# Two transformer-like blocks in one kernel: layer edges rearranged (broadcast wait, late tiles, first units in two parts)

## The reference

```python
def second_block(x, pre_norm_w, post_norm_w, even_w_in, even_w_out, odd_w_in, ...):
    for layer in range(DEPTH):
        h = rms_norm(x, pre_norm_w[layer])
        if layer % 2 == 0:
            y = even_mixer(h, even_w_in[e], even_w_out[e])
        else:
            y = odd_mixer(h, odd_w_in[o], odd_w_out[o], ...)
        x = x + rms_norm(y, post_norm_w[layer]).astype(x.dtype)
    return x
```

## Time and profile before

| | |
|---|---|
| median of 3 runs | 2850.13 us (2848.59 to 2850.41) |
| profiled execution, its own time | 2852.63 us |
| its span | 2850.8 us |
| TensorE matmul busy | 2599.5 us, 91%, 16315 instructions |
| VectorE busy | 1450.0 us, 51% |
| ScalarE busy | 1227.6 us, 43% |
| GpSimd busy | 229.9 us, 8% |
| mean granted TensorE clock | 0.961 |

### The profile page before, as it was taken

The page is one execution under the profiler, slowest core; times in us unless marked ns, Lnnn a source line. Parts: engine busy times, 40 slices in busy tenths (PEclk is TensorE's granted clock), DMA queues, the critical chain, the costliest instruction groups (busy, mean ns, idle before and its releaser), DMA issues. The chain is left out here.

```text
span 2850.8 us, 42051 instructions
## 1 busy us (share of the span) xinstructions
PE 2599.5 (91%) x16315; PEld 2107.5 (74%) x16315; DVE 1450.0 (51%) x2412; ACT 1227.6 (43%) x2306; POOL 229.9 (8%) x300
## 2 busy tenths in 40 slices
PE   5999999999999999988889899999998989997677
PEld 4778987777777989877768688785335877887666
DVE  5122266666656414577766424413776655247642
ACT  6112344454544311366653522213666647225642
POOL 1000020010020000001100000000000100007500
PEclk8999999999999999999999999999999999996779
DMA  7430000000122010100003220101001211010012
GB/s 259 167 128 23 32 18 1 1 1 1 60 82 104 31 45 31 60 2 2 1 7 113 74 89 1 60 30 45 1 1 52 105 41 45 30 64 26 1 46 80
DMA packets 71125, 139.55 MB, mean 49 GB/s; under 512 B 2729, under 2 KB 37954, under 8 KB 70802
## 3 DMA queue, kind: packets, MB, share of 16 engines
q1 hardware_dynamic: 53856, 75.89, 7.8%
q0 software_dynamic: 16832, 60.90, 5.8%
q10 hardware_dynamic: 242, 0.07, 0.0%
HBM read 120.08 MB, written 16.78 MB: 48 GB/s over the span
## 5 line engine op out<-in xcount | busy, mean ns | idle before, releaser
L163 ACT ACTIVATE WORK<-PS 128x512 f32<-128x512 f32 (+5 forms) x307 | 151.6, 494 | 634.4 <-PE PS L794 396.0
L794 PE MATMUL PS<-HT_R,W_R 128*128 128x512 f32 (+1 forms) x864 | 328.5, 380 | 0.0
L792 PE MATMUL PS<-WORK_R,W_R 128*128 128x512 f32 (+1 forms) x640 | 245.1, 383 | 28.0 <-issue 17.9
L793 PE MATMUL PS<-WORK_R,W_R 128*128 128x512 f32 (+1 forms) x704 | 266.5, 379 | 0.0
L163 DVE TENSOR_REDUCE SM<-PS 128x1 f32<-128x1280 f32 (+3 forms) x180 | 199.1, 1106 | 94.8 <-PE PS L1087 49.4
L909 PE MATMUL PS<-WORK_R,HT_R 128*128 128x512 f32 x544 | 217.1, 399 | 21.1 <-DVE W_R L163 20.1
L794 PE MATMUL PS<-W_R,WORK_R 128*128 128x256 f32 (+3 forms) x704 | 215.2, 306 | 0.0
L911 PE MATMUL PS<-W_R,HT_R 128*128 128x512 f32 x544 | 214.1, 394 | 0.0
L910 PE MATMUL PS<-WORK_R,MIXT_R 128*128 128x512 f32 x544 | 213.9, 393 | 0.0
L793 PE MATMUL PS<-W_R,HT_R 128*128 128x256 f32 (+2 forms) x688 | 206.2, 300 | 0.0
L163 ACT ACTIVATE HT<-PS 128x512 f32<-128x512 f32 (+7 forms) x211 | 123.7, 586 | 186.4 <-PE PS L840 111.9
(11 more groups left out here) (291 smaller groups left out, 5682.8 us busy)
## 6 DMA issues: line engine op xcount, KB each, us to landing
MIXT<-in_w_mod POOLq DMA_DIRECT2D x8, 2048.0 KB, 8.4
x_scratch<-WORK POOLq DMA_DIRECT2D x24, 512.0 KB, 2.9
WORK<-x_scratch POOLq DMA_DIRECT2D x24, 512.0 KB, 3.5
W<-in_odd_w_in SPq DMA_DIRECT2D x12, 1024.0 KB, 5.2
W<-in_o_w_in SPq DMA_DIRECT2D x10, 1024.0 KB, 5.1
W<-in_even_w_in SPq DMA_DIRECT2D x5, 2048.0 KB, 8.9
W<-in_w_mod SPq DMA_DIRECT2D x4, 2048.0 KB, 21.2
WORK<-in_x POOLq DMA_DIRECT2D x16, 512.0 KB, 8.1
```

What stands on the lines that cost most here:

```text
L163: self.last = Signalled(self, issue(*args, **kwargs))
L792: mm(out, a[0], b_[0], start=k == 0, stop=False)
L793: mm(out, a[1], b_[0], start=False, stop=False)
L794: return mm(out, a[0], b_[1], start=False, stop=k == KT - 1)
```

## The change

Three edits, all in the three `boundary` functions and the first units behind them.

- DVE's wait for `bcast_in` moves from the head of `boundary` to the first tile, behind its wait for x.
- At edge 2, in the last tile's turn, tile five's high and low part and tile six's eviction move between the steps of the last tile; the high parts of tiles six and seven stay ahead of `first` on ACT. At edge 3 on ACT, `first` (the eviction of an l_x unit) moves behind all late tiles.
- The two units over tiles five to eight run as `split_two`: both banks open, first the 256 columns of tiles five and six for both, then those of tiles seven and eight. Part 0 waits for tile six's low part, part 1 for tile eight's. At edge 3 the first two units over tiles one to four are taken one ahead of the last tile's transposes and one behind.

```diff
+            def split_two(b, keys, name, fs, g, bys):
+                c0, _ = TGL[g]
+                banks = [open_unit(pe, key, by) for key, by in zip(keys, bys)]
+                for part in range(2):
+                    c = c0 + 256 * part
+                    h_split(b, c // P + 1)
+                    for f, bank in zip(fs, banks):
+                        for k in range(KT):
+                            slab_split(name, k)
+                            w = slice(f * P, (f + 1) * P)
+                            o = second_high[b] + 512 * k + 256 * part
+                            last = three_passes(bank[:, 256 * part:256 * part + 256], (high_of(name)[:, k, w], low_of(name)[:, k, w]),
+                                                (WORK_R[:, o:o + 256], HTR[:, k, c:c + 256]), k)
+                        if part:
+                            finish_unit(last)
...
                     x_transposes(b, tiles[-2])
                     first()
                     x_transposes(b, tiles[-1])
+                    if then:
+                        then()
...
             def r_gate_units(n, g):
                 name = ("r_gate", "s_gate")[n // 2]
+                if n == 0 and g:
+                    split_two(2, [(name, r, TGL[g][0]) for r in range(2)], f"{name}0", (0, 1), g, ("act", "act"))
+                    return
...
             def l_x_units(half_n, g):
+                if half_n == 0 and g:
+                    split_two(3, [("l_x", r, TGL[g][0]) for r in range(2)], "l_x0", (0, 1), g, ("dve", "act"))
+                    return
...
-            boundary(3, "r_out", lambda: l_x_units(0, 0))
+            def l_x_first(r):
+                split_t(3, ("l_x", r, TGL[0][0]), "l_x0", r, 0, "act" if r else "dve")
+
+            boundary(3, "r_out", lambda: l_x_first(0), then=lambda: l_x_first(1))
...
+                    last = b == 2 and i == tiles[-1]
+                    if last:
+                        pe_read(act, ("y", b, i, 1))
+                        h_split_high(b, tiles[4])
                     if b == 2:
                         norm_stat(bound_at[b, i])
+                    if last:
+                        x_evict(b, tiles[n - 2])
                     if b < 4:
                         norm_stat(bound_at[b, i])
-                    if n >= 2 and b < 4:
+                    if n >= 2 and b < 4 and not last:
                         x_evict(b, tiles[n - 2])
...
                     if b == 2:
-                        for i in late[:-1]:
+                        for i in late[1:-1]:
                             h_split_high(b, i)
-                    if first:
                         first()
                     x_evict(b, tiles[-1])
...
                     if b:
                         h_split_high(b, tiles[-1])
+                    if b == 3:
+                        first()
...
-                if b >= 2:
-                    dve.wait_ge(bcast_in, 16 * (b - 1))
...
                     dve.wait_ge(x_in[n % 2], 16 * x_loads(n))
+                    if b >= 2 and k == 0:
+                        dve.wait_ge(bcast_in, 16 * (b - 1))
...
                         if b == 2:
+                            if i == tiles[-1]:
+                                h_split_low(b, tiles[4])
                             from_act()
                             link(v.reciprocal(SM[:, 85:86], rms_of(n)))
                             give(v.scalar_tensor_tensor(x, x, SM[:, 85:86], GB[1], ALU.mult, ALU.mult))
+                            if i == tiles[-1]:
+                                x_evict(b, tiles[k - 2])
...
-                    if k >= 2 and b < 4:
+                    if k >= 2 and b < 4 and not (b == 2 and i == tiles[-1]):
                         x_evict(b, tiles[k - 2])
...
                     if b in (1, 2):
-                        for i in late[:2] if b == 1 else late[:-1]:
+                        for i in late[:2] if b == 1 else late[1:-1]:
                             h_split_low(b, i)
```

## The result

The changed kernel takes 2825.98 us (median of 4 runs, 2822.38 to 2831.44) beside 2849.83 us for the kernel before (4 runs, 2848.59 to 2850.41): a ratio of 0.9919 with a 95% interval of 0.9899 to 0.9938, so 18 to 29 us less. Two later sets on other occasions gave 2826.05 beside 2849.69 and 2826.24 beside 2849.68. The profiled execution took 2823.19 us with a span of 2821.4 (before: 2852.63 and 2850.8).

A forecast was written before the change was run, and what follows sets the result against it. TensorE was taken to bound the kernel, busy nine tenths of the span, with reachable pauses at layer edges. Gains of 8.35 + 9.8 + 6.9 = 25.05 us from the 2850.13 median gave 2825.1 us, range 2818 to 2832.

The forecast's parts named there:

- Step 1: Starts of edges 3 and 4: waiting for the broadcast at its use saves 4.1 and 4.25 us, 8.35 in all.
- Steps 2 and 3 at edge 2: End of edge 2: late tiles' work moved into the last tile's waits, and units in two parts, gain 9.8 us.
- Step 3 at edge 3: End of edge 3: one unit before the last tile's transposes, one behind, then two parts of 256 columns, gain 6.9 us.
- The sum: Whole kernel: 8.35 at two starts, 9.8 at edge 2's end and 6.9 at edge 3's end make 25.05 us.
- The clock: Ends of edges 2 and 3 lose a slow start of 2 us each; starts of edges 3 and 4 keep theirs.
- (a): Starts of edges 3 and 4 give nothing because something behind the row is late too: 2833.5 us, chance 0.05.
- (b): Two-part units: narrow matmuls are paced by their weight loads, 0.19 us each: 2837.2 us, chance 0.04.
- (c): Two-part units at both ends: weight loads not hidden at all, 0.31 us a matmul: 2860.7 us, chance 0.02.
- (d): Chunk chain gets a low clock throughout, 27 us at half cover by its waits: 2852 us, chance 0.04.
- (e): Two-part units: the parts still wait for the last tile, so no gain: 2850 us, chance 0.03.

The follow-up runs named there:

- the slab edit: Changed kernel with edge 3's last eviction behind the first two late tiles' parts, and first weight slab split before the first tile at edges 3 and 4: 2822.17 us.
- the wait alone: Kernel before with only VectorE's wait for the broadcast row moved to the row's first use, at all edges: 2841.16 us beside 2850.17.
- run 256: Not a run label: words from "the widths that were run 256 columns"; 256 columns is the part width of the changed kernel, 2825.98 us beside 2849.83.

## Why the prediction was right

Forecast 2825.1 us, measured 2825.98. By its steps:

- **Step 1** (8.35 us): 4.11 at edge 3, from 2171.45 to 2152.93 less the 14.41 that the kernel was ahead at the stick stage's last matmuls; 4.26 off the pause at edge 4. Pauses 3.79 and 4.19 for 3.8 and 4.2. That TensorE wouldn't be starved by ScalarE's and VectorE's slabs held.
- **Steps 2 and 3 at edge 2** (9.8 us): 9.4. Moved to the clock of before (5.06 later, by the first unit), part 0 began at 1603.3, part 1 at 1609.7, the next unit at 1616.0, for 1603.0, 1609.5 and 1615.6. The gain came out 0.4 smaller because the parts are longer than I had summed: without the pause they take 12.3 us to the next unit, not 11.9. Counting 0.12 a matmul leaves out what the starts and the end cost besides (the first spacing behind a pause is 0.19 or 0.23, and the step to the next unit 0.58). Edge 2's order was right down to who ends it: ScalarE's table load, two gate evictions, eviction and last high part hold VectorE 2.49 us ahead of its last low part (ScalarE, then VectorE):

```profile
1597.93 1.28 ACT L163 ACT_TABLE_LOAD   x1
1599.23 1.29 ACT L163 ACTIVATE MIXT<-PS 128x512 f32<-128x512 f32 x2
1600.61 1.57 ACT L163 ACTIVATE HT<-PS,VC 128x128 f32<-128x128 f32 x4
1602.29 1.06 ACT L163 ACTIVATE WORK_R<-HT 128x1024 fp32r<-128x1024 f32 x1
```

```profile
1596.72 2.56 DVE L163 TENSOR_TENSOR HT_R<-HT,WORK_R 128x1024 fp32r<-128x1024 f32 x2 [0.19 <-ACT WORK_R L163]
1599.38 1.51 DVE L163 TENSOR_SCALAR HT<-PS,VC 128x128 f32<-128x128 f32 x4
1603.38 1.23 DVE L163 TENSOR_TENSOR HT_R<-HT,WORK_R 128x1024 fp32r<-128x1024 f32 x1 [2.49 <-ACT WORK_R L163]
```

- **Step 3 at edge 3** (6.9 us): 6.5, with pauses of 0.57, 1.92 and 0 for 0.9, 1.7 and 0. On the clock of before (18.88 later, by the first transposes) part 0 began at 2282.5 for 2282.2; the rest is the parts' own length again, 12.05 for 11.9.
- **The sum** (25.05): the places give 4.11 + 4.26 + 9.4 + 6.48 = 24.2, the medians of three sets 23.4 to 23.9. The difference lies for the most part in step 1. The profiled execution of before had its longest waits at both starts: in the executions that still had the wait at the head, TensorE's pause was 7.49, 7.57 and 7.61 at edge 3 and 8.00, 8.10 and 8.28 at edge 4, for 7.90 and 8.45. The broadcast lands when it lands, and I had read its latest case. And at edge 4 the half pace lasts a little longer behind the shorter pause: the first 48 matmuls take 12.85 to 12.91 us with the wait moved, 12.49 to 12.71 with it at the head. From the last transposes of the chunk chain to the end of the span it is 114.26 to 114.49 us in the four traces with the wait at the head and 110.59 to 110.65 in the seven with it moved, without the slab edit: 3.6 to 3.9 us, not 4.25.
- **The clock** was right in kind. Both ends lost their slow starts; the starts of edges 3 and 4 kept half pace in every traced execution. Two things in its argument were off. The 2 us that I charged to a slow start came from 10.85, which leaves out the step to the next unit: 96 such matmuls at full pace take 22.33 us from unit to unit, so about 11.5 for 48 as an estimate (22.33 less 48 x 0.226), and the half pace cost about 1.6 us at edge 2 (13.07) and 1.9 at edge 3 (13.36), and in the units taken whole again 1.3 and 1.6 (12.8 and 13.05). And edge 4's start, which I named as evidence that a pause of 8.45 makes a slow start, is none: the clock was at half before that pause began.
- **The rivals.** (a) fell with the wait alone; (b) and (c) with the spacing of 0.12. The 0.19 of (b) isn't the load's pace at any width; there is a floor close below 0.12, of 0.111, so of the widths that were run 256 columns is the narrowest that pays (0.6 us more for the two units, 12.05 for about 11.5). (d) didn't come: the chunk chain went at 0.71. Against (e) part 0 starts at 1598.20, before VectorE even evicts the last tile (1599.38).

## What to carry to other kernels

A unit that waits for the last of several remainders can be cut along its columns, so that its first part waits for the first of them; here that was worth more (6.5 and 3.5 us) than the new orders (2.9 and 3.0), and at these two ends it also left no pause that was followed by a slow start. The price is more matmuls, and it must be read from the spacing of that width: 256 columns cost 0.12 for half of 0.226, 128 columns 0.111 for a quarter. And a wait at the head of a step belongs at the first instruction that reads what it waits for.

## What the runs showed of the hardware

- A matmul of 128 columns in the rounded type, each with its own load of 128x128, is started every 0.111 us at full clock (four parts of 128 columns); of 256 columns every 0.12, of 512 every 0.226.
- At edges 2 and 3, where the clock was full before the pause, these pauses stood ahead of half pace: 3.07, 3.57, 3.79, 4.45, 7.27, 7.49 to 7.61, 7.90, 7.94, 9.89 and 9.93 us. Pauses of 0.3 to 1.98 us there never did. Behind 3.79 us the start at 2152.93 of after opened with a matmul of 0.47, ran its first two at full pace and only from 2153.84 at half (0.43 each), to 2156.83.
- The pause's length alone doesn't decide. A pause of 3.19 or 3.20 us ahead of the same matmuls near 920 us was followed by half pace in ten of twelve executions and by full pace in two. And elsewhere shorter pauses do stand ahead of half pace: 2.22 us at 1807.45 of after, where TensorE had run only four matmuls of 128 columns since the pause of 2.40 us before. The rows are before, then the third execution of the kernel after, at the one place:

```profile
926.32 0.50 PE L792 MATMUL PS<-W_R,MIXT_R 128*128 128x256 f32 x1 [3.20 <-DVE W_R L163]
926.62 0.41 PE L793 MATMUL PS<-W_R,HT_R 128*128 128x256 f32 x1
```

```profile
923.10 0.36 PE L792 MATMUL PS<-W_R,MIXT_R 128*128 128x256 f32 x1 [3.20 <-DVE W_R L163]
923.29 0.28 PE L793 MATMUL PS<-W_R,HT_R 128*128 128x256 f32 x1
```

- The same instructions ahead of edge 1 took 781.20 to 788.00 us in twelve executions of ten kernels, a scatter larger than the smallest of the effects studied.
